# Attention steps in a hybrid decoder trunk: the weighted sum ahead of the row maximum, outputs copied out as an item begins, and steps placed on more items

## The reference

```
u = rmsnorm(x) @ w_in                       # split into LRU input, gate, q, k, v
lru_out = scan(conv(xl), gates) * gelu(gl)
w = softmax(q1 k1') - lam * softmax(q2 k2') # 4 heads, causal, two softmaxes per head
o = rmsnorm(w @ v) * (1 - lam_init)
x = x + rmsnorm(concat(lru_out, o) @ w_out)
x = x + rmsnorm((silu(h @ w_gate) * (h @ w_up)) @ w_down)     # h = rmsnorm(x), 2816 wide
x = x + rmsnorm(sigmoid(x @ ple_w_gate) * (p @ ple_w_proj))
```

## Time and profile before

| | |
|---|---|
| median of 3 runs | 3170.92 us (3169.41 to 3175.09) |
| the profiled execution, its own time | 3174.06 us |
| its span, first to last instruction | 3172.3 us |
| mean granted TensorE clock | 0.968 of full |
| busy: PE, DVE, ACT, POOL | 94%, 56%, 43%, 7% |
| `feed` from its first item with a tick to the last | about 955 to 2475 us of the span |

### The profile page before, as it was taken

The page is one execution under the profiler, slowest core; times in us unless marked ns, Lnnn a source line. Parts: engine busy times, 40 slices in busy tenths (PEclk is TensorE's granted clock), DMA queues, the critical chain, the costliest instruction groups (busy, mean ns, idle before and its releaser), DMA issues.

```text
span 3172.3 us, 38465 instructions
## 1 busy us (share of the span) xinstructions
PE 2966.4 (94%) x14384; PEld 2413.3 (76%) x14384; DVE 1779.2 (56%) x2858; ACT 1375.5 (43%) x2500; POOL 220.2 (7%) x314
## 2 busy tenths in 40 slices
PE   6999999759999999999999999899999999999997
PEld 5788787547768777777877787778788777787875
DVE  5767745357626666566565556655666555333454
ACT  4655635344224444554444445544444444222233
POOL 0101100110000000001000100001111000000000
PEclk9999989868999999999999999999999999999998
DMA  5546332546754443454443334534332244232221
GB/s 159 182 140 222 133 134 73 150 135 228 217 150 116 123 113 113 154 159 120 116 114 105 108 101 155 162 103 130 100 114 76 96 167 126 80 97 84 86 74 59
DMA packets 377720, 402.65 MB, mean 127 GB/s; under 512 B 25657, under 2 KB 277989, under 8 KB 377536
## 3 DMA queue, kind: packets, MB, share of 16 engines
q1 hardware_dynamic: 360768, 341.38, 36.5%
q0 software_dynamic: 16768, 58.81, 4.8%
HBM read 341.26 MB, written 58.91 MB: 126 GB/s over the span
## 4 chain that ended last, share of the span: by engine, by line
PE 60%; DVE 11%; ACT 3%; issue 2%; DMA 0%; SPq 0%; DVEq 0%; ACTq 0%; POOL 0%; POOLq 0%
PE c_bank L2582 48%; PE b_S L2874 3%; PE b_WT L2886 2%; DVE c_w L2262 2%; PE b_O L2900 2%; DVE b_m L2462 1%; PE b_S L2591 1%; PE b_O L2591 1%; ACT c_junk L2034 1%; DVE c_rows L2273 1%; DVE c_rows L2280 1%; PE b_S L2854 1%; PE b_O L2902 1%; DVE c_act L2374 1%; DVE b_p L2469 1%
## 5 line engine op out<-in xcount | busy, mean ns | idle before, releaser
L2582 PE MATMUL c_bank<-c_hT,c_w 128*128 128x512 f32 (+1 forms) x4416 | 1036.8, 389 | 14.9 <-DVE c_hT L2300 14.9
L2582 PEld LDWEIGHTS c_bank<-c_hT,c_w 128*128 128x128 f32 x4416 | 802.0, 192 | 171.9 <-issue 17.7
L2262 DVE TENSOR_TENSOR c_w<-c_raw,c_w 128x1024 fp32r<-128x1024 f32 x334 | 405.5, 1220 | 198.2 <-ACT c_w L2013 196.9
L2582 PE MATMUL c_bank<-c_w,c_fT 128*128 128x512 f32 x2112 | 506.7, 393 | 0.0
L2013 ACT ACTIVATE c_w<-c_raw 128x1024 fp32r<-128x1024 f32 x334 | 351.1, 1055 | 290.2 <-PE c_bank L2582 246.3
L2582 PEld LDWEIGHTS c_bank<-c_w,c_fT 128*128 128x128 f32 x2112 | 391.7, 188 | 87.3 <-issue 3.4
L2191 ACT ACTIVATE b_p<-b_S,b_nm 128x512 f32<-128x512 f32 (+3 forms) x288 | 180.0, 630 | 518.6 <-DVE b_nm L2463 518.6
L808 PE MATMUL a_bank<-a_w,a_hT 128*128 128x512 f32 (+1 forms) x1224 | 300.1, 401 | 0.0
L2582 PE MATMUL c_bank<-c_w,c_hT 128*128 128x512 f32 x1152 | 270.4, 393 | 7.7 <-DVE c_w L2262 4.0
L808 PEld LDWEIGHTS a_bank<-a_w,a_hT 128*128 128x128 f32 (+1 forms) x1224 | 220.6, 183 | 61.3 <-issue 3.8
L2582 PEld LDWEIGHTS c_bank<-c_w,c_hT 128*128 128x128 f32 x1152 | 217.9, 190 | 54.8 <-DVE c_w L2262 4.4
(11 more groups left out here) (362 smaller groups left out, 3391.2 us busy)
## 6 DMA issues: line engine op xcount, KB each, us to landing
c_raw<-in_ffn_w_gate SPq DMA_DIRECT2D x88, 512.0 KB, 4.9
c_raw<-in_ffn_w_up SPq DMA_DIRECT2D x88, 512.0 KB, 4.1
c_raw<-in_ffn_w_down SPq DMA_DIRECT2D x88, 512.0 KB, 4.3
a_raw<-in_w_in SPq DMA_DIRECT2D x40, 1024.0 KB, 5.1
b_k<-split_kT SPq DMA_DIRECT2D x72, 256.0 KB, 4.9
b_v<-split_v SPq DMA_DIRECT2D x36, 512.0 KB, 3.6
c_raw<-in_w_out SPq DMA_DIRECT2D x32, 512.0 KB, 5.0
c_raw<-in_ple_w_gate SPq DMA_DIRECT2D x32, 512.0 KB, 4.4
```

What stands on the lines that cost most here:

```text
L2262: V.tensor_tensor(w[:, e[1] % SLOTS, 1], raw[:, n % RAW], w[:, e[1] % SLOTS, 0].bitcast(F32), ALU.subtract).then_inc(split_ready, 1)
L2582: ins = T.matmul(out, lhs(k, a), rhs(k, b), start=first and k == 0 and n == 0, stop=end and k == blocks - 1 and n == 2)
```

## The change

Four edits. (1) In `attend_first`, DVE's weighted sum of step t - 4 is issued ahead of the row maximum of step t. (2) In `feed`, DVE's weighted sum is likewise issued ahead of the row maximum. (3) In `feed`, the copy of O (ACT) and the sum of its halves (DVE) go from the end of an item to its start; the square sum and root go ahead of the high part of an activation on ACT. (4) `PLACES` takes in the "down" items of the third part in every group (before: of group 0 alone) and the "pg" items of the first half: 171 places where there were 153, for the same 150 ticks.

The diff, cut to its core:

```
 # attend_first, DVE
             for t in range(END):
+                s = t - ADD
+                if 0 <= s < NSTEP:
...
+                    dve.wait_ge(t2_ready, s + 1)
+                    V.scalar_tensor_tensor(p[...], p[...], coef[...], p[...], ALU.mult, ALU.add).then_inc(w_ready, 1)
                 if t < NSTEP:
                     dve.wait_ge(s_done, t + 1)
                     link(V.reduce_max(m[...], S[t % 2][...], axis=AX))
...
-                s = t - ADD
-                (the same lines)
 # feed, places
-    PLACES = [n for n, (i, item) in enumerate(ALL) if i < LAST and item[0] in ("gate", "up", "down") and item[:2] != ("down", 2)]
+    PLACES = [n for n, (i, item) in enumerate(ALL) if i < LAST and (item[0] in ("gate", "up", "down") or item[:2] == ("pg", 0))]
-    PLACES = sorted([n for n in PLACES if n > FINISH + 3] + [at[0, ("down", 2, 0, kp)] for kp in range(3)])
+    PLACES = [n for n in PLACES if n > FINISH + 3]
 # feed, ACT, at the start of an item
+                x = finished(n, 1)
+                if x is not None:
+                    act.wait_ge(pv_done, last_step[x] + 1)
+                    wait_if_any(act, o_ready, x)
+                    A.activation(ob[:], O[:, 0, 1], ACT.Copy).then_inc(ob_ready, 1)
                 if was == ("mix0", 3):
...
 # feed, ACT, at the end: taken out there, and the square sum and root go ahead of
                 if was[0] in ("up", "far"):
...
                     A.activation(fT[:, b % 8, 0], act1[:, b % 2], ACT.Copy).then_inc(f_hi, 1)
 # feed, DVE, at the start of an item
+                x = finished(n, 1)
+                if x is not None:
+                    dve.wait_ge(ob_ready, x + 1)
+                    if x >= 4:
+                        dve.wait_ge(o_turned, x // 4)
+                    V.tensor_tensor(o[:, x % 4], O[:, 0, 0], ob[:], ALU.add).then_inc(o_ready, 1)
 # feed, DVE: weighted sum (wait t2_ready) now ahead of reduce_max (wait s_done)
```

More of the change, by code:

```diff
@@ L1239, in _ @@
             for t in range(END):
+                s = t - ADD
+                if 0 <= s < NSTEP:
+                    i, kc, n = tile_of[s], STEPS[s][3], size(s)
+                    dve.wait_ge(t2_ready, s + 1)
+                    V.scalar_tensor_tensor(p[:, s % PRING, 0, 0:n], p[:, s % PRING, 0, 0:n], coef[:, i % TRING, 0, kc:kc + 1],
+                                           p[:, s % PRING, 1, 0:n], ALU.mult, ALU.add).then_inc(w_ready, 1)
                 if t < NSTEP:
@@ L2200, in _ @@
                     A.activation(wT[:, 0, 0:size(s)], WT[:, 0:size(s)], ACT.Copy).then_inc(wt_hi, 1)
[L2201 to L2205, removed]
                 x = finished(n, 1)
                 if x is not None:
-                    act.wait_ge(pv_done, last_step[x] + 1)
-                    wait_if_any(act, o_ready, x)
-                    A.activation(ob[:], O[:, 0, 1], ACT.Copy).then_inc(ob_ready, 1)
                     act.wait_ge(o_ready, x + 1)
@@ L2216, in _ @@
                         A.activation(oss[:], oss[:], ACT.Sqrt, bias=eps[:, 2:3], scale=1.0 / P).then_inc(ostd_ready, 1)
+                if was[0] in ("up", "far"):
+                    b = was[1]
+                    bank, count = job[j, "up", b]
+                    act.wait_ge(acc_free[bank], count)
+                    A.activation(fT[:, b % 8, 0], act1[:, b % 2], ACT.Copy).then_inc(f_hi, 1)
                 if n == SOFT + 1:
@@ L2454, in _ @@
                         V.nop().then_inc(so_free, 1)
+                s = valued(n)
+                if s is not None:
+                    g, h, t, kc = STEPS[s]
+                    x, c = tile_no(g, h, t), size(s)
+                    dve.wait_ge(t2_ready, s + 1)
+                    V.scalar_tensor_tensor(p[:, s % PRING, 0, 0:c], p[:, s % PRING, 0, 0:c], coef[:, x % TRING, 0, kc:kc + 1],
+                                           p[:, s % PRING, 1, 0:c], ALU.mult, ALU.add).then_inc(wc_ready, 1)
                 s = scored(n)
@@ L2463, in _ @@
                     V.tensor_scalar(nm[:, x % TRING, :, kc], m[:, x % TRING, :, kc], -QSCALE, None, ALU.mult).then_inc(nm_ready, 1)
[L2464 to L2470, removed]
                 s = scored(n)
@@ L2486, in _ @@
                 x = finished(n, 1)
[L2487 to L2491, removed]
                 s = scored(n)
```

## The result

The changed kernel took 3195.10 us (median of 4 runs, 3189.94 to 3200.23) against 3170.44 of the kernel before beside it (3169.41 to 3175.09). The ratio is 1.0075, with an interval of 1.0056 to 1.0094: slower by 24.7 us. The forecast was slower, 3191 us.

What follows compares the result with a forecast made beforehand. PE, busy 94% of the span, was taken as the bound, so only its stands count: 89.5 us lost after against 69 before, +20 us on the 3170.92 median, 3191 us; range 3150 to 3210.

Steps and rivals of the forecast that it cites:

- The prices per item: Tile ends with edit 3: 0.57 behind gate or inner down blocks, 1.49 behind up, 2.32 behind finished down blocks.
- T0: Moment, from an item's scores' start, when DVE is free for the step; value products wait T0 - 2.03 after the change.
- unhindered item: Item where PE waits for nothing before its ending head's turn: transposes at 3.73, value products at 6.95 from the scores' start.
- 39.2: Loss in us put on 37 tile ends in three classes: 12.0 behind gate/inner down, 17.9 up, 9.3 finished down.
- The items of a head's turn: Items behind a turn: 1.1 lost seven times, 3.4 three times, 18 us; the turn's own waits 17.3 against 12.5.
- the clock: Granted-clock dips at head's turns: about two left, 3 us, against four items and 7.4 us before.
- the 0.25 that an item behind an up block was said to cost beyond its wait: Kernel before: transposes 0.89 late with a 0.71 us wait, so some 8 us more over 33 items.
- The place: Head of the ACT and DVE streams: the waiting copy of O holds up tanh and weight split behind it.
- The first rival: Faster: the copy at ACT's stream head delays nothing that counts, T0 under 2.03 behind gate blocks; -18, 3153 us; chance 0.17.
- an item that only this edit touches gains at most 0.43: Weighted sum first: loss goes from T0 - 1.60 to T0 - 2.03 as the wait moves to the value products.
- a price of 6 us for nine ticks in "pg" items: Edit 4: DVE's weighted sum meets the normalisation's work, between 0 and 1.5 per tick, taken as 0.7.
- The slower rival: Clock falls at ten more turns and items behind them, with stands of 2.3 to 3.7, 1.6 each; 3207 us; chance 0.13.

Runs made afterwards that it cites:

- run 7: Changed kernel with O's copy and the halves' sum moved behind the item's tanh, activation products and weight splits: 3152.16 us, ratio 0.9932 to the kernel before.
- run 2: The second edit alone (weighted sum ahead of the row maximum in feed), on the kernel before: 3178.19 us, ratio 1.0020.
- run 1: Changed kernel with the third edit undone, copy and sum of the halves back at the item's end: 3172.85 us, ratio 1.0002 to the kernel before.

## Why the prediction was right, and what in it was not

**The prices per item held.** T0 was put at 2.60, 3.52 and 4.35; the timeline has 2.60 to 2.63 in 12 of the 21 items behind gate and inner down blocks (2.70 to 3.08 in the other nine), 3.54 in nearly all behind up blocks and, behind a finished down block, 4.24 in three of the four. Taken over all items of a class, the value products start later than the 6.92 of an unhindered item by 16.1 us in the 21 (12.0 was said), 16.3 in 11 behind up blocks (17.9 for 12), and 8.9 in the 4 behind finished down blocks (9.3). The sum is 41.3 against 39.2. The items of a head's turn lost 19 (18 was said), their transposes waited 14.8 (17.3), and none of them the 3.7 that was said of one. The value products wait for the low part 50 times (some 40 were said), but by 0.6 at the most and not by up to 2.5: behind up and finished down blocks a part of the lateness is had at the transposes already.

**That the sum lies within 1 us of the stage's 21.3 is in part luck.** No term holds the 0.10 us by which the second value product starts later behind a wait, 5 us over 50 of them, and the gate class cost 4 more than was said; the turns' waits, the clock and the up class cost less. And the 0.25 that an item behind an up block was said to cost beyond its wait is 0.18 by its own row (0.89 less 0.71), 6 us over the 33 and not 8.

**The place was right.** In the kernel after, the tanh and the split that needed nothing of O started behind the waiting copy, after an idle time of 2.60 and 2.44 us on ACT. The Trainium skill (PSUM — Partial Sum Buffer, Engine vs sequencer instructions) says that the queues of ScalarE, VectorE and GpSimdE are strictly first in, first out. These traces agree with it. In run 7 the same work without the wait ahead of it ran early, and the time fell by 43 us.

**The first rival named a real kernel.** It said that if the copy delayed nothing that counts, the time would be 3153. The change didn't do that, but run 7 does, by order alone, at 3152. Its condition, T0 under 2.03 behind a gate block, is what the order decides: 19 of the 21 items behind gate and inner down blocks meet it in run 7 (0.72 to 1.88), none in the kernel after.

**What was wrong is the worth of weighted sum first by itself.** The step "an item that only this edit touches gains at most 0.43" counted two limits, the transposes and the low part, and left out a third: where a tile ends, the value products also need the sum of the halves, which stood behind the low part. In such an item edit 2 makes a loss, and alone it cost 6.6 us (run 2). Hence the edits don't add: alone they measure nothing, +6.6, +56 and -4.3 us, together +24.7. Edit 3 works both ways in the whole: by the sums above it costs some 41 us at the head of the queue, and it spares the wait for O that edit 2 makes (15.6 us in run 1); taking it away gained 22, near the 25 that this leaves. The sum came out right since in the changed kernel the outputs are read out early and that limit does not bind; a forecast for edit 2 alone would have had the wrong sign.

**Edit 4** was taken as moving tile ends and head's turns away from up blocks, at a price of 6 us for nine ticks in "pg" items. Its sign holds on both sides (-4.3 alone, and 10 us worse when undone in the whole), each time only just clear of noise. Without it the transposes wait 26.6 us in place of 21.5, and the mean granted clock is 0.967 to 0.968 in the four runs, against 0.971 in three of the four with it.

**The clock** took less than the 3 us that were said. Three turns have a dip where two were foretold: one behind an up block, with a stand of 2.45 us, and two behind gate blocks, with stands of 2.09. They cost about 1 us: the latter two items last 9.13 and 9.69 us against 9.02 and 9.33 of two like ones at full clock, and in the first the value products come 0.8 later than T0 and the full clock give, by estimate. The slower rival took stands of 2.3 to 3.7 for the size at which the clock falls; the turns in group 0 with 2.18 and 2.30 kept it (last section).

**Open.** The profiles differ by 15.9 us and the medians by 24.7. The stage's 21.3 lies between, but which part of the other executions was longer wasn't seen.

## What to carry to other kernels

In an in-order stream, an instruction that waits belongs behind the work that does not need what it waits for; here the order of one copy and one sum, with the same instructions, was worth 43 us. Before a step is put later on an engine, list everything behind it there and what buffer each of those frees: the wait for the buffer (O) appeared under a different name than the wait that was removed. And edits that move work ahead should be priced in pairs, since one may only pay with the other.

## What the runs showed of the hardware that was not expected

The granted clock fell after some stands of PE at a head's turn and not after others of the same length. The windows of four items of the kernel after (length, busy us of PE, PEld, DVE, ACT and POOL, PEclk, DMA share, GB/s). The first two, ("up", 7) and ("up", 10) of group 1, open behind a stand of 2.09 us; the third has a stand of 2.18 us before its transposes of the weights, the fourth one of 2.45:

```profile
1505.67:1514.69 9.02, 8.29 (x44) 6.46 (x42) 4.78 (x7) 6.29 (x10) 1.82 (x2) 1.00 0.25 90
1616.86:1625.99 9.13, 9.13 (x42) 7.50 (x41) 4.68 (x6) 6.28 (x10) 1.82 (x2) 0.85 0.28 88
1041.29:1050.25 8.96, 6.78 (x37) 5.45 (x35) 4.55 (x10) 5.32 (x11) 0.59 (x1) 1.00 0.37 117
1826.96:1839.24 12.28, 9.83 (x46) 7.83 (x44) 7.05 (x10) 7.18 (x12) 2.29 (x4) 0.86 0.28 89
```

The first kept the full clock of 2.4 GHz. The second, behind as long a stand, was granted 0.85 on the mean, a stretch of it at the lower level of 1.2 GHz. The third kept the full clock, the fourth did not. In the kernel before, the item of the earlier trace rows kept it through a stand of 3.68 (the first window of the earlier trace rows), while four others with stands of 3.66 to 3.78 had the dip. So in these traces the length of the one stand does not decide; what does was not tried.
